# The inverse kept in its PSUM bank, its level factors copied on ScalarE

## What is computed

```python
def step(s, inp):
    r_t, w_t, k_t, v_t, kk_t, a_t = inp
    sa = jnp.einsum('bhvk,bhk->bhv', s, kk_t)
    s = (s * w_t[:, :, None, :] - sa[..., None] * (kk_t * a_t)[:, :, None, :]
         + v_t[..., None] * k_t[:, :, None, :])
    return s, jnp.einsum('bhvk,bhk->bhv', s, r_t)
```

## Time and profile before

| what | us |
|---|---|
| time, median of 3 runs (lowest, highest) | 1237.46 (1235.92, 1238.48) |
| the profiled execution's own time | 1235.28 |
| its span in the profile | 1233.6 |
| PE busy | 1126.9 |
| PEld busy | 1009.9 |
| DVE busy | 683.0 |
| ACT busy | 394.3 |
| POOL busy | 373.8 |
| mean granted clock of TensorE, share of full | 0.965 |

### The profile page before, as it was taken

One profiled execution on the slowest core, in us unless ns is written; L12 is line 12 of the kernel. 1 busy time (PEld: TensorE's weight loads), 2 busy tenths in 40 slices (PEclk: granted clock), 3 DMA queues, 4 the chain that ended last, 5 costly groups with the idle time before them and its releaser, 6 DMA issues. The chain is left out here.

```text
span 1233.6 us, 36488 instructions
## 1 busy us (share of the span) xinstructions
PE 1126.9 (91%) x16691; PEld 1009.9 (82%) x16691; DVE 683.0 (55%) x937; ACT 394.3 (32%) x706; POOL 373.8 (30%) x326
## 2 busy tenths in 40 slices
PE   4869998999889999995899999999999999869997
PEld 0369887899869988975899999999999999646686
DVE  0561004948746222255677777778787877374542
ACT  3331100101113233223354344444434443253321
POOL 6161111111303222313333334334534444041110
PEclk9979998999989999997899999999999999979999
DMA  9501233211102201000000000000000000180121
GB/s 375 174 1 35 69 108 107 69 35 44 60 1 73 79 29 35 1 1 10 3 4 13 4 3 4 4 4 3 4 4 4 4 3 4 63 315 35 69 103 52
DMA packets 29974, 61.76 MB, mean 50 GB/s; under 512 B 3296, under 2 KB 21364, under 8 KB 28666
## 3 DMA queue, kind: packets, MB, share of 16 engines
q1 hardware_dynamic: 28332, 54.17, 12.7%
q10 hardware_dynamic: 1488, 5.24, 1.1%
HBM read 49.68 MB, written 9.73 MB: 48 GB/s over the span
## 5 line engine op out<-in xcount | busy, mean ns | idle before, releaser
L609 PE MATMUL ps<-input_rounded,weights_rounded 128*128 128x386 f32 x768 | 266.3, 347 | 10.2 <-DVE zc L779 5.2
L611 PE MATMUL ps<-input_rounded,weights_rest 128*128 128x386 f32 x768 | 262.2, 341 | 0.0
L610 PE MATMUL ps<-input_rest,weights_rounded 128*128 128x386 f32 x768 | 262.2, 341 | 0.0
L1261 POOL TENSOR_TENSOR arena<-arena,lvl 128x512 f32<-128x512 f32 x108 | 136.3, 1275 | 206.9 <-DVE arena L1340 105.9
L609 PEld LDWEIGHTS ps<-input_rounded,weights_rounded 128*128 128x128 f32 x768 | 147.0, 191 | 18.4 <-issue 12.6
L610 PEld LDWEIGHTS ps<-input_rest,weights_rounded 128*128 128x128 f32 x768 | 146.8, 191 | 0.9 <-issue 0.6
L611 PEld LDWEIGHTS ps<-input_rounded,weights_rest 128*128 128x128 f32 x768 | 146.9, 191 | 0.0
L412 POOL TENSOR_TENSOR weights_rest<-arena,weights_rounded 128x2048 fp32r<-128x2048 f32 x16 | 75.6, 4722 | 209.8 <-ACT weights_rounded L458 209.8
L1014 PE MATMUL ps<-arena 64*64 64x64 f32 x2880 | 103.2, 221 | 17.6 <-DVE arena L1358 16.4
L1014 PEld LDWEIGHTS ps<-arena 64*64 64x64 f32 x2880 | 94.0, 137 | 20.7 <-DVE arena L1358 20.7
L1006 PE MATMUL ps<-arena 64*64 64x64 f32 x2880 | 104.1, 221 | 6.2 <-issue 3.4
(11 more groups left out here) (227 smaller groups left out, 1958.4 us busy)
## 6 DMA issues: line engine op xcount, KB each, us to landing
arena<-in_w_in SPq DMA_DIRECT2D x16, 1024.0 KB, 5.4
arena<-in_ada_w SPq DMA_DIRECT2D x12, 1024.0 KB, 6.8
mix_scratch<-zc SPq DMA_DIRECT2D x4, 1158.0 KB, 9.2
out<-arena SPq DMA_DIRECT2D x9, 512.0 KB, 2.6
zc<-in_x_sample ACTq DMA_DIRECT2D x2, 2048.0 KB, 20.5
zc<-in_w_out SPq DMA_DIRECT2D x4, 1024.0 KB, 8.4
arena<-in_x_sample SPq DMA_DIRECT2D x8, 512.0 KB, 3.3
zc<-mix_scratch SPq DMA_DIRECT2D x1, 2316.0 KB, 18.2
```

The costliest lines, as they stand in the source:

```text
L609: pe.matmul(o, w_hi[:, k, cut], hi_of_h[:, k, cols_b], start=(k == 0), stop=False)
L610: pe.matmul(o, w_hi[:, k, cut], lo_of_h[k][:, cols_b], start=False, stop=False)
L611: last = pe.matmul(o, w_lo[:, k, cut], hi_of_h[:, k, cols_b], start=False, stop=(k == KT - 1))
L1261: pool.tensor_tensor(flat(Um[l % 3]), TA[n % 2][:, :, :, 0, :].rearrange("p d a c -> p (d a) c"), lvl[:, l, :].unsqueeze(1).to_broadcast([ ...
```

## The change

- `update` no longer overwrites bank 1 but adds to it (start=False). `factor` gives minus the product in place of eye minus it, and so Y is not multiplied anew but corrected where it stands.
- Bank 1 is filled by a new `seed` on ACT, which copies Y into it, once for each chunk. Update 1 waits for it.
- One matmul with start=True opens the bank, once, ahead of the loop.
- `factor` moves from DVE to ACT.
- ACT's order within a step is now: stage_lora, **factor 1**, copy_y 1, decay_tanh, rate_tanh, **factor 2**, negate_rhs, key_factor, copy_y 2, copy_u, **factor 3**, exps, copy_y 3, rate, **factor 4**, chunk_decay, copy_y 4, **factor 5**, copy_y 5, v_by_token, keys_by_token, **seed**.
- DVE's order is the old one less its five factors. PE's order is the old one.

```diff
                 def update(n, l):
                     pe.wait_ge(q_F, 5 * n + l)
                     earlier(pe, q_Y, 5 * n + l - 1)
+                    if l == 1:
+                        pe.wait_ge(q_seed, n + 1)
                     for d, a in BLOCKS_OF:
                         for r in HALVES:
-                            last = pe.matmul(bank(1)[r, d, a, :], PX[r, d, a, :], Y[r, d, a, :], start=True, stop=True)
+                            last = pe.matmul(bank(1)[r, d, a, :], PX[r, d, a, :], Y[r, d, a, :], start=False, stop=True,
+                                             skip_group_check=True)
                     last.then_inc(q_Q, 1)
...
                 pe.wait_ge(q_init, 1)
+                pe.matmul(ps[:, 1, :], eye[:, :], keep, start=True, stop=True).then_inc(q_open, 1)
...
+                def seed(n):
+                    act.wait_ge(q_Y0, n + 1)
+                    if n == 0:
+                        act.wait_ge(q_open, 1)
+                    earlier(act, q_Y, 5 * n)
+                    act.activation(bank(1), Y, ACT.Copy).then_inc(q_seed, 1)
+
+                def factor(n, l):
+                    act.wait_ge(q_P, 5 * n + l)
+                    earlier(act, q_Q, 5 * n + l - 1)
+                    act.activation(PX, bank(0), ACT.Copy, scale=-1.0).then_inc(q_F, 1)
...
                     if A:
                         stage_lora(na)
+                    if L:
+                        factor(nl, 1)
+                        copy_y(nl, 1)
+                    if A:
                         decay_tanh(na)
                         rate_tanh(na)
                     if L:
-                        copy_y(nl, 1)
+                        factor(nl, 2)
                     if Z:
                         negate_rhs(nz)
                     if A:
                         key_factor(na)
+                    if L:
+                        copy_y(nl, 2)
                     if Z:
                         copy_u(nz)
-                    if L:
-                        copy_y(nl, 2)
...
+                    if L:
+                        factor(nl, 3)
                     if A:
                         exps(na)
+                    if L:
+                        copy_y(nl, 3)
+                    if A:
                         rate(na)
                     if L:
-                        copy_y(nl, 3)
+                        factor(nl, 4)
+                    if A:
+                        chunk_decay(na)
+                    if L:
                         copy_y(nl, 4)
-                    if A:
-                        chunk_decay(na)
-                    if L:
+                        factor(nl, 5)
                         copy_y(nl, 5)
                     if A:
                         v_by_token(na)
                         keys_by_token(na)
+                        seed(na)
...
-                def factor(n, l):
-                    dve.wait_ge(q_P, 5 * n + l)
-                    earlier(dve, q_Q, 5 * n + l - 1)
-                    dve.tensor_tensor(flat(PX), eye8(), flat(bank(0)), ALU.subtract).then_inc(q_F, 1)
-
```

More of the change, by code:

```diff
@@ L873, in hybrid_step_kernel @@
         q_F = sem2("level_factor")
+        q_seed = sem2("inverse_seeded")
+        q_open = sem2("inverse_bank_opened")
         q_Q = sem2("level_update")
@@ L1226, in _ @@
                         act.activation(sio, bank(3), ACT.Copy).then_inc(q_fc, 1)
+                    if L:
+                        factor(nl, 3)
                     if A:
                         exps(na)
+                    if L:
+                        copy_y(nl, 3)
+                    if A:
                         rate(na)
                     if L:
-                        copy_y(nl, 3)
-                        copy_y(nl, 4)
+                        factor(nl, 4)
                     if A:
@@ L1235, in _ @@
                     if L:
+                        copy_y(nl, 4)
+                        factor(nl, 5)
                         copy_y(nl, 5)
@@ L1391, in _ @@
                     if L:
-                        factor(nl, 1)
                         transpose_x(nl, 1)
@@ L1396, in _ @@
                         add_bias(na, 1)
-                    if L:
-                        factor(nl, 2)
                     if A:
@@ L1406, in _ @@
                     if L:
-                        factor(nl, 3)
                         transpose_x(nl, 3)
@@ L1410, in _ @@
                         queries(na)
-                    if L:
-                        factor(nl, 4)
                     if A:
@@ L1422, in _ @@
                         mask(na, 0, q_gT, TA, q_mT)
-                    if L:
-                        factor(nl, 5)
                     if A:
```

## The result

1302.73 us, median of 4 runs (1300.65 to 1304.3), against 1237.97 of the kernel before beside it: ratio 1.0522, 95% interval 1.0498 to 1.0546. The change costs 65 us. The profiled execution took 1302.17 us, 66.9 more than the 1235.28 of the one profiled before.

A forecast was written before the change was run, and what follows sets the result against it. TensorE's order of passes and its stalls were taken to bound the kernel. 48 + 16 + 28 = 92 us on 1235.3 gave 1327, or 1329 against the runs' median; the range ran from 4 us below 1301 to 1357.

The forecast's parts named there:

- What bounds the kernel: Whole scan: TensorE's own order of passes sets the step; relieving VectorE is worth nothing by itself.
- Factor 5 behind the decay copies: Before update 5: factor 5 waits behind copies held by decay_state; net 3.0 us in each of 16 steps, 48 us.
- The 0.23: Step's turn: product 1's present 0.23 us wait for the transpose comes back, reducing update 5's 3.26 us delay.
- Seed ahead of factor 1: Step's turn: seed and stage_lora precede factor 1, so update 1 comes 0.95 us later in 17 steps, 16 us.
- the prediction's sentence from the Trainium skill: Seed's copy: the skill calls ScalarE's way to PSUM faster, by which the 16 us term would be somewhat smaller.
- near 80 us in all: Profile after: update's waits for ScalarE's factor, about 3.2 us in 16 steps and 1.7 in 17, where 16.4 stood.
- The covers: Rest of the step: later factors and rate stay hidden; gram_b has only 0.5 us to spare.
- The clock: TensorE after the stalls: one half-rate stretch in each of 16 steps, 28 us; clock from 600 us about 0.94.
- rival (a): TensorE's clock holds; the same two stalls cost 48 + 16 = 64 us, 1301; chance 0.22.
- (c): The stall before update 5 does not arise; only the turn costs, 16 us, 1254; chance 0.04.
- (d): Faster: relieved VectorE and factor 1 on idle ScalarE shorten the turn, 5 to 17 us, 1220 to 1232; chance 0.05.
- Busy times: Profile after: VectorE's falls by 61.5 us for 90 factors; ScalarE's grows by 0.6 for each of 108 copies.

The follow-up runs named there:

- run 3: Kernel after, with chunk_decay put back behind factor 5 and stage_lora issued in the middle of the step before: 1238.35 us, ratio 1.0011 to the kernel before.
- run 1: Kernel after, with chunk_decay put back behind factor 5, ahead of copy_y 5: 1261.06 us, ratio 1.0198 to the kernel before.
- run 2: Kernel after, with stage_lora of the next chunk issued behind factor 4, in the middle of the step before: 1309.7 us, ratio 1.059 to the kernel before.
- run 4: Kernel before, with only chunk_decay put ahead of copy_y 4 and no factor moved: 1296.45 us, ratio 1.0488.
- run 6: Kernel after, with two or four short unread ScalarE copies added ahead of factor 5: 1320.97 us with two, 1336.95 us with four.
- run 7: Kernel after, both ScalarE waits mended, first lora product before update 1, inverse begun ahead of decay_state, decay copies behind next step's copy_y 1: 1222.85 us, ratio 0.9874.
- run 8: Kernel before, lora product before update 1, stage_lora early; first kernel also inverse ahead of decay_state, decay copies moved: 1226.96 us; second without those two: 1228.45 us.

## Why the prediction was right, and where it was not

- **What bounds the kernel**: right. TensorE's order plus its stalls makes the time, and relieving VectorE brought nothing that could be measured by itself (run 3).
- **Factor 5 behind the decay copies**, 3.0 us in 16 steps, 48: measured from transpose_v's start, update 5 comes after 4.03 us (823.65 to 827.68) where it came after 0.93 before (820.73 to 821.66), so 3.10 late, less 0.23 is 2.87 a step, 46 us. The bracket of 2.88 is smaller than 3.10 because it counts from the modelled end of the pass ahead. The 0.23 went as foreseen: product 1 at 830.53 has no bracket. Update 5 starts 1.4 us after decay_state's end, as in the sum; decay_state ended 0.1 us sooner than I put it (2.61 after transpose_v's start, before 2.73). 42 us came back in run 1, which by the table gave 3 us of its gain to the clock.
- **Seed ahead of factor 1**, 0.95 us in 17 steps, 16: measured 2.98 from product 1 to update 1 (830.53 to 833.51) where it was 1.93 (824.91 to 826.84), 1.05 a step, 18. The edit that took stage_lora out took 17.3 us of waiting away, so it is stage_lora more than the seed that the change put on the path; no run took the seed out with stage_lora left in place. From the seed's start to stage_lora's it is 0.52 us (831.24 to 831.76), where I took 0.50. So this term did not come out smaller, as the prediction's sentence from the Trainium skill would have it (the page, ScalarE: Activation LUTs, has that in its section Step-by-step: what each stage is for). That TensorE would wait near 80 us in all was met to 0.3, in part by luck: the first stall was 0.3 us shorter than forecast and the second 0.2 longer.
- **The covers**: held. VectorE waited for b_keys (22.3 us in 17 times, 1.3 each), and gram_b still came on time but for one wait of 0.6, beside its first one of 8.3 us, which was 8.1 before. The 0.5 us of room was enough.
- **The clock**, 28 us: the term that was mis-sized for this change. It was to fall once in each of 16 steps. It fell in 5 stretches, 20.5 us, against one of 10.2 before, which is 5 us net. None of the five is that of before, in the second step; there the clock held this time. The mean granted clock from 620 to 1040 us was 0.98, not 0.94. So the forecast of 1329 was 26 too high. The measured time is that of rival (a), 1301, to which I had given 0.22, and it lay in the range because the range took (a) in. That it lies so near is luck in part: (a) wants a clock that holds, and it fell five times. The mechanism is real: one stretch per step is what runs 2 and 4 show, 36 and 26 us of their time by the table. What I had wrong is what decides. I argued from the length of the stall. But run 4 and the kernel after show the opposite order: 2.5 us with the clock low in 15 of 16 steps, and 2.9 and 1.9 us with the clock at 1.00 for 340 us.
- **The Trainium skill**, page TensorE: Matmul & The Clock Gate, Part 1, has idle time throttle the clock and activity release it. The traces agree with both halves: 0.52 behind 2.5 idle us, then 1.00 after 3.5 busy ones (run 4). In run 1 stalls of 1.9 us were enough. That each stall of this size does it was my step and not the page's, and the traces speak against it.
- **What stays open**: why the kernel after is spared. Within run 6 a stall longer by 0.3 and 0.6 us took the low stretches from 5 to 12 and 18, so length may have a part. It can't be the whole: neither the stall's length nor the sum of both stalls orders the runs of the table, equal stalls in one execution had different outcomes, and executions of one kernel in run 6 differed by 16 us. That points to where in time the stalls fall. No run moved the steps without changing them, so this is argued and not shown.
- **Rivals (c) and (d)**: fell by the same rows. That (d) leads nowhere is plain from run 3. The stalls of the turn could be had (run 7), but through TensorE's order, with no faster factor.
- **Busy times**: ScalarE's grew by 61.8 us, not 65; VectorE's fell by 54.9, not 61.5. Its 18 prefix scans got 0.5 us longer each (below), 9.1 in all, but two of its products by the decays got shorter by 7.9 together. Summed row by row it lost 59.8; rows that overlap count once in busy time, and the other 4.9 I put down to that.

## What to carry to other kernels

When work moves to another engine's list, read what its new neighbours wait for. The factor's price was 0.6 us wherever it stood; its place behind a copy that waits for a late state cost 2.9 us a step, and 42 us in all. Put an instruction with a late release and a late reader behind everything that the bounding engine needs, and stage inputs early, in the middle of the step, where the engine idles. If an engine is bound by its own order, fill its one latency gap with an independent product first: that gave most of 1%, and no other edit here gave more than a few tenths of one. Price stalls on TensorE with and without a clock stretch behind them, as two cases; a mended stall can give nothing back when the clock falls elsewhere.

## What the runs showed of the hardware that I had not expected

- The same kernel can differ by 16 us from run to run through the granted clock alone (1313 to 1329, at 0.958 to 0.946), when its stalls bring the clock down in some steps and not in others.
- A ScalarE copy from SBUF to a bank takes 597 ns for 128x512, as long as one from a bank (583 to 597 by line in the kernel after). The nearest from SBUF to SBUF is a tanh, 630.
- VectorE's SBUF work beside GpSimd's is slow here, and by how much goes with the overlap. decay_state took 1.75 us where GpSimd's three masks covered its first 1.2 us (821.71 to 822.91), 1.23 in its new place in run 8, where a mask covered its first 0.7 (818.46 to 819.14), and 0.68 at the scan's end with GpSimd idle. In the kernel before:

```profile
819.19 3.72 POOL L1261 TENSOR_TENSOR arena<-arena,lvl 128x512 f32<-128x512 f32 x3 [6.79 <-DVE arena L1340]
...
1060.32 0.68 DVE L1374 TENSOR_TENSOR arena<-arena 128x512 f32<-128x512 f32 x1
```

In the kernel after, the prefix scan begins 0.5 us sooner after product 2 and runs beside the whole of a mask, and takes 2.33 us where it took 1.80 with 0.7 us beside a mask:

```profile
807.08 2.33 DVE L1337 TENSOR_TENSOR_SCAN arena<-arena 128x512 f32<-128x512 f32 x1 [0.46 <-ACT arena L1150]
...
807.06 1.27 POOL L1290 TENSOR_TENSOR arena<-arena,lvl 128x512 f32<-128x512 f32 x1 [4.82 <-PE ps L1008]
```

It cost nothing here, since the transpose behind it waits for update 2 anyway.
